# Inverting the chunk triangles of a gated DeltaNet in 32x32 tiles of TensorE

## The chip, the cores and the metric

One core of a Trainium2 chip. The metric is the device time of one execution in microseconds (us). Matmuls are float32 throughout. In the traces a float32 matmul leaves two pairs of records, a weight load (PEld) and a pass (PE) each; a transpose leaves one pair.

## The reference

One transformer layer for 2048 tokens of width 1024: modulation from a condition vector, one combined projection, a mix of latent attention (8 heads) and gated DeltaNet (4 heads of 128), an output projection, and a mixture of experts. The change is in the DeltaNet part, which solves a triangular system for each chunk of tokens and each head:

```python
lower = jnp.where(strict, jnp.einsum('bhncd,bhnsd->bhncs', k_beta, k) * decay, 0.0)
system = lower + jnp.eye(C, dtype=lower.dtype)
rhs = jnp.concatenate([v_beta, k_beta * jnp.exp(g)[..., None]], axis=-1)
sol = lax.linalg.triangular_solve(system, rhs, left_side=True, lower=True)
...
o_c = jnp.einsum('bhcd,bhde->bhce', q_c, state) + jnp.einsum('bhcs,bhse->bhce', a_c, v_new)
state = state * jnp.exp(gl_c)[..., None, None] + jnp.einsum('bhcd,bhce->bhde', kd_c, v_new)
```

The reference has chunks of 64 tokens. The kernel works on 16 chunks of 128 tokens, which gives the same outputs, so it inverts a unit triangular 128x128 matrix for each of 16 chunks and 4 heads.

## The kernel before

The kernel runs as stages one after another: `modulation`, `projection`, `mix`, `output`, `routing`, `experts`, `finish`. Only `mix` is touched. It does the attention and the DeltaNet together.

`mix_order` writes out one order of work. DeltaNet steps of chunk n (named K, KA, U0, W0, Y, WU, ...) stand in a list, each with a cost; attention atoms (S scores, X exponential, T transposes of the probabilities, V values, O output transposes) have costs of their own, 495.9 units in all. After each DeltaNet step so many atoms follow as its cost times a share pays for; the share is the sum of the atoms' costs over the sum of the steps' costs (380 units before). Every engine walks through this same order and does its part of each step. Within an engine the order is strict; between engines there are semaphores.

The steps of the inversion, for chunk n and all four heads at once (tiles of 128 partitions x 4 heads x 128):

- K: TensorE multiplies keys and queries (L1194), VectorE makes `lt` ("A_transposed", L1055), and GpSimd multiplies `lt` by the mask of each of seven levels into `xt` ("X_transposed", L905), 3 levels at K and the others after Y steps.
- U0: VectorE sets `U = I - X0` (L1068). W0: TensorE transposes U in 4 transposes (L1216), ScalarE copies it to `W` (L961).
- Levels 1 to 6, each in two steps. Y: 4 matmuls `X^T W` (L1226), ScalarE copies the result to `Y_all` (L965). WU: 4 matmuls for the update of W (L1235, levels 1 to 5 only) and 4 for that of U (L1238); VectorE subtracts both from `W` (L1089) and `U` (L1091).
- TR uses U: `vn = U^T R` (L1244), and the recurrence goes on with DS (L1250) and AV (L1255).

Other lines that the prediction names: M, one step a chunk, has four matmuls in column tiles of 32 (L1261); V has its two heads in column tiles of 64 (L1288); S is L1273, T is L1278. `at_bank` gives each step one or two of five PSUM banks.

Of the kernel before, what the change touches and what calls it, by code (L numbers as in the profile page):

```python
# [22 lines left out]
P = 128  # L23
F32, I32 = mybir.dt.float32, mybir.dt.int32
ALU = mybir.AluOpType
# [589 lines left out]
def mix_order():  # L615

    pairs = [(i, hp, b) for i in range(NT) for hp in range(AH // 2) for b in range(i // 4 + 1)]
    atoms = []
    for j, (i, hp, b) in enumerate(pairs):
        n = min(4, i + 1 - 4 * b)  # L620
        ahead = min(4, pairs[j + 1][0] + 1 - 4 * pairs[j + 1][2]) if j + 1 < len(pairs) else 0
        for e in range(2):
            atoms.append((0.11 * n, [("T", j, e)]))
            if ahead:
                atoms.append((0.22 * ahead, [("S", j + 1, e), ("X", j + 1, e)]))
        o = j - pairs.index((i, 0, 0))
        if i and o < AH // 2:
            atoms.append((0.11 * ((i - 1) // 4 + 1), [("O", i - 1, o)]))
        atoms.append((0.22 * n, [("V", j, 0)]))
        if i and o == AH // 2 - 1:  # L630
            atoms.append((0.0, [("A", i - 1, 0)]))
        if (hp, b) == (AH // 2 - 1, i // 4):
            atoms.append((0.0, [("B", i, 0)]))
    for o in range(AH // 2):
        atoms.append((0.44, [("O", NT - 1, o)]))
    atoms.append((0.0, [("A", NT - 1, 0)]))
    steps = []
    for c in range(-2, NT):
# [4 lines left out]
        steps += [(0.0, ("U0", n)), (0.7, ("W0", n)), (1.2, ("Y", n, 1))] * prep  # L643
# [3 lines left out]
        steps += [(1.35, ("WU", n, 2)), (1.2, ("Y", n, 3))] * prep  # L647
        steps += [(0.0, ("UTA", d))] * (d < NT)
        steps += [(1.35, ("WU", n, 3))] * prep
# [5 lines left out]
        steps += [(1.35, ("WU", n, 5))] * prep  # L655
        steps += [(0.0, ("O2", c))] * rec
        steps += [(1.2, ("Y", n, 6)), (0.5, ("WU", n, 6))] * prep
# [17 lines left out]
def mix(nc, m, a_log, dt_bias, w_mod, b_mod):  # L675

    LV = 7
    NLV = LV - 1
# [9 lines left out]
    with nc.cleanup_on_exit(), ExitStack() as ctx:  # L688
# [8 lines left out]
        masks = sb("level_masks", [P, LV, P])  # L697
# [4 lines left out]
        xt = sb("X_transposed", [P, 3, GH, P])  # L702
        U = [sb(f"U{i}", [P, GH, P]) for i in range(2)]
        at = [sb(f"qk_transposed{i}", [P, GH, P]) for i in range(2)]
        W, Y = sb("W_all", [P, GH, P]), sb("Y_all", [P, GH, P])
# [33 lines left out]
        xw_ready, y_copied, w_ready, u_ready, w_updated, u_updated = (sem(n) for n in (  # L739
            "xw_ready", "y_copied", "w_ready", "u_ready", "w_updated", "u_updated"))  # L740
# [12 lines left out]
        uses = {"G": 1, "K": 2, "VT": 1, "KD": 1, "KS": 2, "W0": 1, "Y": 1, "WU": 2, "TR": 1, "DS": 1, "AV": 1, "M": 1, "PRE": 2, "T": 1, "O": 1}  # L753
# [3 lines left out]
        for step in order:  # L757
            kind, n = step[0], step[1]
            if kind not in uses:
                continue  # L760
            lv = step[2] if len(step) > 2 else 0
            count = 1 if kind == "WU" and lv == NLV else uses[kind]
            held = sorted(range(NBANK), key=until.__getitem__)[:count]
            at_bank[step] = held
            bank_free[step] = [released[b] for b in held if released[b]]
            read = {"G": [(dm_ready, n + 1)], "K": [(at_ready, n + 1)] * 2, "VT": [(v_copied, n + 1)], "KD": [(kd_ready, n + 1)],
                    "KS": [(r_ready, n + 1), (qs_ready, n + 1)], "W0": [(w0_copied, n + 1)], "Y": [(y_copied, NLV * n + lv)],
                    "WU": [(u_updated, NLV * n + lv), (w_updated, (NLV - 1) * n + lv)], "TR": [(vn_ready, n + 1)],
                    "DS": [(state_ready, n + 1)], "AV": [(o_ready, n + 1)], "M": [(mod_added, n + 1)],
                    "PRE": [(pre, 14)] * 2,  # L770
                    "T": [(t_copied[lv % 2], n + 1)], "O": [(part_ready, n * (AH // 2) + lv + 1)]}[kind]
# [96 lines left out]
        def _(pool):  # L868
# [9 lines left out]
            for lv in range(LV):  # L878
# [16 lines left out]

            def level(n, lv):

                t = LV * n + lv
                if lv == 0:
                    wait(lt_ready, n + 1)  # L900
                if lv >= 3:
                    wait(u0_ready, n + 1) if lv == 3 else wait(xw_ready, NLV * n + lv - 3)
                else:
                    wait(xw_ready, NLV * (n - 1) + lv + 4)
                pool.tensor_tensor(xt[:, t % 3], lt[:], masks[:, lv].unsqueeze(1).to_broadcast([P, GH, P]), ALU.mult).then_inc(xt_ready, 1)  # L905

            for step in order:
# [26 lines left out]
        def _(act):  # L934
            wait = waiter(act)
            act.preload_act_table_set("natural_log_exp_and_others")
            for step in order:
# [20 lines left out]
                elif kind == "W0":  # L958
                    wait(w0_ready, n + 1)
                    wait(u_updated, NLV * n)  # L960
                    act.copy(W[:], bank[at_bank[step][0]][:]).then_inc(w0_copied, 1)  # L961
# [46 lines left out]
        def _(dve):  # L1008
# [3 lines left out]
            for step in order:  # L1012
# [36 lines left out]
                elif kind == "K":  # L1049
                    wait(kk_ready, n + 1)  # L1050
                    wait(em_ready, n + 1)
                    wait(xt_ready, n * LV)
# [4 lines left out]
                    last.then_inc(lt_ready, 1)  # L1057
                elif kind == "KA":
# [6 lines left out]
                elif kind == "U0":  # L1065
                    wait(xt_ready, n * LV + 1)
                    wait(tr_ready, n - 1)
                    dve.tensor_tensor(U[n % 2][:], m.ident[:].unsqueeze(1).to_broadcast([P, GH, P]), xt[:, (LV * n) % 3], ALU.subtract  # L1068
# [106 lines left out]
        def _(pe):  # L1175
            wait = waiter(pe)
            for step in order:
# [35 lines left out]
                elif kind == "W0":  # L1213
                    wait(u0_ready, n + 1)
                    for h in range(GH):
                        last = pe.transpose(bank[b0][:, h], U[n % 2][:, h], m.ident[:])  # L1216
                    last.then_inc(w0_ready, 1)
                elif kind == "Y":
                    lv = step[2]
                    wait(xt_ready, n * LV + 1 + lv)  # L1220
                    if lv == 1:
                        wait(w0_copied, n + 1)
                    else:
                        wait(w_updated, (NLV - 1) * n + lv - 1)
                    for h in range(GH):
                        last = pe.matmul(bank[b0][:, h], xt[:, (LV * n + lv) % 3, h], W[:, h], start=True, stop=True)  # L1226
                    last.then_inc(xw_ready, 1)
                elif kind == "WU":
                    lv = step[2]
                    wait(y_copied, NLV * n + lv)  # L1230
                    if lv > 1:
                        wait(u_updated, NLV * n + lv - 1)
                    if lv < NLV:
                        for h in range(GH):
                            last = pe.matmul(bank[b1][:, h], U[n % 2][:, h], Y[:, h], start=True, stop=True)  # L1235
                        last.then_inc(w_ready, 1)
                    for h in range(GH):
                        last = pe.matmul(bank[b0][:, h], Y[:, h], U[n % 2][:, h], start=True, stop=True)  # L1238
                    last.then_inc(u_ready, 1)
                elif kind == "TR":  # L1240
                    wait(r_ready, n + 1)
                    wait(u_updated, NLV * (n + 1))
# [829 lines left out]
```

## Time and profile before

| | |
|---|---|
| median of 3 runs | 2852.04 us (2846.66 to 2852.78) |
| the profiled execution | 2850.87 us, its span 2849.1 us |
| TensorE busy | 2533.8 us, 89% of the span |
| VectorE, ScalarE, GpSimd busy | 41%, 30%, 19% |
| granted TensorE clock, mean | 0.957 of 2.4 GHz |

The span is the time from the first to the last instruction of the profiled execution. The stage `mix` runs from about 800 to 1825 us of it. Busy time of TensorE is from the start of a pass to its modelled end, and passes overlap, so the price of an instruction is read from the distance between starts.

### The profile page before, as it was taken

How to read it: one execution, taken by the hardware profiler on the slowest of the kernel's cores; microseconds unless marked ns; L12 is line 12 of the kernel's file. 1: busy time of each engine (PE TensorE's matmuls, PEld its weight loads, DVE VectorE, ACT ScalarE, POOL GpSimd, SP SyncE). 2: the span in 40 equal slices, each digit the busy share in tenths (PEclk: the TensorE clock that was granted, in tenths of full speed). 3: DMA queues.
4: the chain of work that ended last, by engine and by line, in shares of the span. 5: the costliest groups of instructions: out<-in, count | busy, mean ns of one | idle time of the engine just before them, and what ended most of it. 6: DMA issues, size and time to landing. Idle time of an engine off the chain costs nothing. (4 is left out here: it accounts for less than half of the span.)

```text
span 2849.1 us, 37400 instructions
## 1 busy us (share of the span) xinstructions
PE 2533.8 (89%) x12276; PEld 1561.0 (55%) x12277; DVE 1167.4 (41%) x2349; ACT 855.6 (30%) x2023; POOL 539.1 (19%) x755
## 2 busy tenths in 40 slices
PE   7699999999959999999999999479993899999980
PEld 7354444444447777777777777345552444444440
DVE  0234334333336666666666656412225222222215
ACT  0225334252344444444444444221110011111102
POOL 0110000000022212221222221013331122222222
PEclk9999999999979999999999999789996899999995
DMA  7212112121163123111112111373330478999878
GB/s 261 75 52 69 54 56 76 35 70 39 50 189 94 60 67 105 62 51 47 51 40 71 62 35 35 135 273 119 118 118 22 128 211 266 286 314 309 233 196 361
DMA packets 194351, 348.60 MB, mean 122 GB/s; under 512 B 20368, under 2 KB 128912, under 8 KB 192032
## 3 DMA queue, kind: packets, MB, share of 16 engines
q1 hardware_dynamic: 180256, 296.39, 30.9%
q0 software_dynamic: 13952, 50.36, 7.3%
q8 instruction: 83, 1.36, 0.2%
q14 instruction: 60, 0.49, 0.1%
HBM read 246.56 MB, written 100.16 MB: 122 GB/s over the span
## 5 line engine op out<-in xcount | busy, mean ns | idle before, releaser
L604 PE MATMUL pV<-h_transposed,w_in_sb 128*128 128x512 f32 x768 | 337.6, 592 | 1.6 <-ACT h_transposed L399 1.6
L1900 PE MATMUL hidden_ps<-w,h_rowsT 128*128 x752 | 331.6, 594 | 0.0
L984 ACT ACTIVATE probs<-scores,neg_max 128x512 f32<-128x512 f32 (+3 forms) x320 | 199.5, 624 | 381.8 <-DVE neg_max L1130 258.9
L1273 PE MATMUL scores<-keys,queries 96*128 96x512 f32 (+3 forms) x640 | 289.2, 534 | 13.3 <-DMA values<-v_d 13.3
L1900 PEld LDWEIGHTS hidden_ps<-w,h_rowsT 128*128 128x128 f32 x752 | 143.3, 191 | 180.3 <-issue 180.2
L604 PEld LDWEIGHTS pV<-h_transposed,w_in_sb 128*128 128x128 f32 x768 | 144.6, 190 | 174.8 <-issue 169.8
L1490 PE MATMUL out_ps<-w_out_sb,yT 128*128 128x512 f32 x512 | 225.7, 599 | 2.2 <-DVE yT L1463 2.2
L905 POOL TENSOR_TENSOR X_transposed<-A_transposed,level_masks 128x512 f32<-128x512 f32 x112 | 141.1, 1272 | 409.0 <-DVE A_transposed L1055 196.1
L1278 PE MATMUL bank<-ident,probs 128*128 128x128 f32 x1088 | 178.9, 280 | 3.6 <-ACT probs L984 2.7
L1130 DVE TENSOR_REDUCE neg_max<-scores 128x1 f32<-128x512 f32 x192 | 132.4, 690 | 105.0 <-PE scores L1273 104.0
L1910 PE MATMUL expert_ps<-w_sb,hiddenT 128*128 x368 | 169.8, 604 | 0.0
L1278 PEld LDWEIGHTS bank<-ident,probs 128*128 128x128 f32 x1088 | 127.2, 141 | 74.4 <-issue 69.4
L1288 PE MATMUL outT_ps<-probs_T,values 128*64 128x128 f32 x2176 | 155.5, 281 | 11.7 <-issue 5.9
L1490 PEld LDWEIGHTS out_ps<-w_out_sb,yT 128*128 128x128 f32 x512 | 96.8, 192 | 118.8 <-issue 116.0
L1830 ACT ACTIVATE silu_gate<-hidden_ps 128x256 f32<-128x256 f32 x47 | 18.1, 385 | 454.4 <-PE hidden_ps L1900 454.4
L1288 PEld LDWEIGHTS outT_ps<-probs_T,values 128*64 128x64 f32 x2176 | 116.9, 137 | 68.5 <-issue 55.8
L1859 DVE TENSOR_TENSOR hidden<-silu_gate,hidden_ps 128x256 f32<-128x256 f32 x47 | 19.8, 422 | 276.3 <-ACT silu_gate L1830 276.3
L522 DVE TENSOR_SCALAR conv_acc<-conv_in,conv_taps 128x512 f32<-128x512 f32 x48 | 23.7, 494 | 243.4 <-ACT conv_in L441 243.4
L1868 DVE SCALAR_TENSOR_TENSOR expert_y<-expert_ps,slot_gate,mod_rows 128x512 f32<-128x512 f32 x92 | 64.8, 747 | 133.2 <-PE expert_ps L1910 133.2
L1273 PEld LDWEIGHTS scores<-keys,queries 96*128 96x128 f32 x640 | 99.8, 194 | 26.5 <-issue 25.0
L560 PE MATMUL pG<-w_in_sb,h_transposed 128*128 128x512 f32 x256 | 112.5, 592 | 0.0
L1226 PE MATMUL bank<-W_all,X_transposed 128*128 128x128 f32 x768 | 104.4, 279 | 7.2 <-ACT W_all L961 4.8
(334 smaller groups left out, 3905.9 us busy)
## 6 DMA issues: line engine op xcount, KB each, us to landing
w<-in_w_dram SPq DMA_DIRECT2D x64, 1024.0 KB, 10.8
w_sb<-in_w_dram SPq DMA_DIRECT2D x32, 1024.0 KB, 14.1
w_mod_rows<-in_w_mod_dram SPq DMA_DIRECT2D x16, 1024.0 KB, 4.8
kqv<-qkv_d SPq DMA_DIRECT2D x16, 768.0 KB, 4.7
y_d<-diag_mask SPq DMA_DIRECT2D x17, 512.0 KB, 6.0
mod_w<-in_w_mod_dram SPq DMA_DIRECT2D x2, 4096.0 KB, 21.7
x_in<-in_x_dram SPq DMA_DIRECT2D x16, 512.0 KB, 3.6
qkv_d<-l_out SPq DMA_DIRECT2D x32, 256.0 KB, 2.3
```

Of the source, the lines that this page charges most:

```text
L560: last = pe.matmul(pG[:], hT[:, n // ST % 2, k, n % ST * P:(n % ST + 1) * P], win[:, k, GATE0:], start=(k == 0), stop=(k == ND - 1))
L604: last = pe.matmul(pV[n % 2][:], win[:, k, QKV0 + c * P:QKV0 + (c + 1) * P], hT[:, s % 2, k, :], start=(k == 0), stop=(k == ND - 1))
L905: pool.tensor_tensor(xt[:, t % 3], lt[:], masks[:, lv].unsqueeze(1).to_broadcast([P, GH, P]), ALU.mult).then_inc(xt_ready, 1)
L984: act.activation(prob[:, e, 0:w].rearrange("p t k -> p (t k)"), pS[e][:, 0:w * P], ACT.Exp, scale=-1.0, bias=nmin[:, i % 2, h, b:b + 1], a ...
L1130: dve.tensor_reduce(nmin[:, i % 2, h, b:b + 1], pS[e][:, 0:w], AX.X, ALU.min).then_inc(min_ready, 1)
L1226: last = pe.matmul(bank[b0][:, h], xt[:, (LV * n + lv) % 3, h], W[:, h], start=True, stop=True)
L1273: pe.matmul(pS[e][:, 0:w * P], qT[:, i % 2, h], kT[:, 4 * b:4 * b + w, h, :], start=True, stop=True).then_inc(s_ready, 1)
L1278: last = pe.transpose(bank[b0][:, t], prob[:, e, t], m.ident[:])
L1288: last = pe.matmul(pO[64 * e:64 * e + 64, n % 4], v[:, 4 * b + t, h * DV:(h + 1) * DV], probT[:, n % 2, e, t], start=(t == 0), stop=(t == ...
L1490: last = pe.matmul(pX[:, half], yT[par][:, k], wo[:, k, half * 512:(half + 1) * 512], start=(k == 0), stop=(k == ND - 1))
L1900: last = pe.matmul(pH[par][:], xT[par][:, k], m.w13[:, ds(slot, 1), k].rearrange("p s n -> p (s n)"), start=(k == 0), stop=(k == ND - 1))
L1910: last = pe.matmul(pY[:, half], hT[par][:, k], m.w2b[:, ds(slot, 1), k, half * 512:(half + 1) * 512].rearrange("p s n -> p (s n)"), start= ...
```

## The change

The inversion of the 128x128 triangle is cut by block size. Levels 0 to 4 stay inside diagonal blocks of 32, so they now work on a compact form: for each head the four diagonal 32x32 blocks stand under each other in 128 partitions x 32 columns. VectorE copies these blocks out of `lt` into `ltb` (four copies), GpSimd makes all five masked levels in two instructions, and TensorE multiplies each block in its own 32x32 tile of the array (rows q and columns q for block q). W and U stand side by side in one tile `WU`, so one subtraction updates both. W0 is a matmul by a compact identity in place of a transpose.

Level 5 joins pairs of blocks of 32 to blocks of 64, level 6 the two of 64 to 128, each on its off-diagonal block alone. A new ScalarE step D copies the finished blocks into the wide `U` and into `Wh`; level 5's result is written by three ScalarE instructions, level 6's by one of VectorE. `U` and `Wh` are zeroed once at the start. The costs of the Y and WU steps in `mix_order` are lowered, so that all steps sum to 307.2 units.

```diff
-        steps += [(1.35, ("WU", n, 1)), (1.2, ("Y", n, 2))] * prep
+        steps += [(0.9, ("WU", n, 1)), (0.8, ("Y", n, 2))] * prep
...
-        steps += [(1.2, ("Y", n, 4))] * prep
+        steps += [(0.8, ("Y", n, 4)), (0.9, ("WU", n, 4)), (0.0, ("D", n))] * prep
         steps += [(0.85, ("G", d))] * (d < NT)
-        steps += [(1.35, ("WU", n, 4)), (1.2, ("Y", n, 5))] * prep
+        steps += [(0.8, ("Y", n, 5))] * prep
...
-    LV = 7
-    NLV = LV - 1
+    NLV = 6
+    LVB, BL = 5, 32
+    quarter = [slice(BL * j, BL * (j + 1)) for j in range(P // BL)]
...  GpSimd
                 elif kind == "K":
-                    for lv in range(3):
-                        level(n, lv)
-                elif kind == "Y" and step[2] + 2 < LV:
-                    level(n, step[2] + 2)
+                    wait(ltb_ready, n + 1)
...
+                    pool.tensor_tensor(xt[:, 0], ltb[:], mask_b[:, 0].unsqueeze(1).to_broadcast([P, GH, BL]), ALU.mult).then_inc(xt_ready, 1)
+                    pool.tensor_tensor(xt[:, 1:], ltb[:].unsqueeze(1).to_broadcast([P, LVB - 1, GH, BL]),
+                                       mask_b[:, 1:].unsqueeze(2).to_broadcast([P, LVB - 1, GH, BL]), ALU.mult).then_inc(xt_ready, 1)
...  ScalarE
-                    act.copy(Y[:], bank[at_bank[step][0]][:]).then_inc(y_copied, 1)
+                    bk = bank[at_bank[step][0]]
+                    if step[2] < LVB:
+                        act.copy(Yb[:], bk[:, :, 0:BL]).then_inc(y_copied, 1)
+                    elif step[2] == LVB:
+                        act.copy(Yb[quarter[1]], bk[quarter[1], :, 0:BL])
+                        act.copy(Yb[quarter[3]], bk[quarter[3], :, 0:BL]).then_inc(y_copied, 1)
+                    else:
+                        act.copy(Yh[64:], bk[64:, :, 0:64]).then_inc(y_copied, 1)
+                elif kind == "D":
...
+                    for q in quarter[0:2]:
+                        act.copy(Wh[q, :, q], WU[q, :, 0])
+                    for q in quarter[2:4]:
+                        last = act.copy(U[n % 2][q, :, q], WU[q, :, 1])
+                    last.then_inc(diag_ready, 1)
+                    for q in quarter[0:2]:
+                        last = act.copy(U[n % 2][q, :, q], WU[q, :, 1])
+                    last.then_inc(diag_ready, 1)
+                elif kind == "WU" and step[2] == LVB:
...
+                    act.activation(Wh[quarter[1], :, quarter[0]], bk[quarter[1], :, 0:BL], ACT.Copy, scale=-1.0)
+                    act.activation(U[n % 2][quarter[2], :, quarter[3]], bk[quarter[2], :, 0:BL], ACT.Copy, scale=-1.0)
+                    act.activation(U[n % 2][quarter[0], :, quarter[1]], bk[quarter[0], :, 0:BL], ACT.Copy, scale=-1.0).then_inc(quarter_done, 1)
...  VectorE
+                    wait(lt_ready, n + 1)
+                    for q in quarter:
+                        last = dve.tensor_copy(ltb[q], lt[q, :, q])
+                    last.then_inc(ltb_ready, 1)
...
-                elif kind == "WU":
-                    lv = step[2]
-                    if lv < NLV:
-                        wait(w_ready, (NLV - 1) * n + lv)
-                        dve.tensor_tensor(W[:], W[:], bank[at_bank[step][1]][:], ALU.subtract).then_inc(w_updated, 1)
-                    wait(u_ready, NLV * n + lv)
-                    dve.tensor_tensor(U[n % 2][:], U[n % 2][:], bank[at_bank[step][0]][:], ALU.subtract).then_inc(u_updated, 1)
+                elif kind == "WU" and step[2] < LVB:
+                    wait(u_ready, NLV * n + step[2])
+                    dve.tensor_tensor(WU[:], WU[:], bank[at_bank[step][0]][:, :, 0:2 * BL].rearrange("p h (two c) -> p h two c", two=2),
+                                      ALU.subtract).then_inc(u_updated, 1)
+                elif kind == "WU" and step[2] == NLV:
+                    wait(u_ready, NLV * (n + 1))
+                    dve.tensor_scalar(U[n % 2][0:64, :, 64:], bank[at_bank[step][0]][0:64, :, 0:64], -1.0, None, ALU.mult
+                                      ).then_inc(half_done, 1)
...  TensorE, Y and WU
                     for h in range(GH):
-                        last = pe.matmul(bank[b0][:, h], xt[:, (LV * n + lv) % 3, h], W[:, h], start=True, stop=True)
+                        if lv < LVB:
+                            for q in quarter:
+                                last = pe.matmul(bank[b0][q, h, 0:BL], xt[q, lv, h], WU[q, h, 0], start=True, stop=True)
+                        elif lv == LVB:
+                            for first, second in (quarter[0:2], quarter[2:4]):
+                                last = pe.matmul(bank[b0][second, h, 0:BL], lt[first, h, second], WU[first, h, 0], start=True, stop=True)
+                        else:
+                            last = pe.matmul(bank[b0][64:, h, 0:64], lt[0:64, h, 64:], Wh[:, h], start=True, stop=True)
...
-                    if lv < NLV:
-                        for h in range(GH):
-                            last = pe.matmul(bank[b1][:, h], U[n % 2][:, h], Y[:, h], start=True, stop=True)
-                        last.then_inc(w_ready, 1)
                     for h in range(GH):
-                        last = pe.matmul(bank[b0][:, h], Y[:, h], U[n % 2][:, h], start=True, stop=True)
+                        if lv < LVB:
+                            for q in quarter:
+                                pe.matmul(bank[b0][q, h, 0:BL], WU[q, h, 1], Yb[q, h], start=True, stop=True)
+                            for q in quarter:
+                                last = pe.matmul(bank[b0][q, h, BL:2 * BL], Yb[q, h], WU[q, h, 1], start=True, stop=True)
+                        elif lv == LVB:
+                            pe.matmul(bank[b0][quarter[1], h, 0:BL], WU[quarter[1], h, 1], Yb[quarter[1], h], start=True, stop=True)
+                            for first, second in (quarter[0:2], quarter[2:4]):
+                                last = pe.matmul(bank[b0][first, h, 0:BL], Yb[second, h], WU[second, h, 1], start=True, stop=True)
+                        else:
+                            last = pe.matmul(bank[b0][0:64, h, 0:64], Yh[64:, h], U[n % 2][64:, h, 64:], start=True, stop=True)
```

## Rows read from the trace of the kernel before

**Rows 1.** The page: busy time, then TensorE and its granted clock in 40 slices.

```profile
PE 2533.8 (89%) x12276; PEld 1561.0 (55%) x12277; DVE 1167.4 (41%) x2349; ACT 855.6 (30%) x2023; POOL 539.1 (19%) x755
...
PE   7699999999959999999999999479993899999980
...
PEclk9999999999979999999999999789996899999995
```

**Rows 2.** Windows: busy us of each engine, granted clock, DMA share; `mix` and its end.

```profile
core 0: us, PE busy (x) PEld busy (x) DVE busy (x) ACT busy (x) POOL busy (x), PEclk, DMA share, GB/s
860.00:1820.00 960.00, 918.59 (x7151) 705.28 (x7151) 614.50 (x1328) 438.80 (x1182) 202.74 (x195) 1.00 0.19 60
1820.00:1880.00 60.00, 14.98 (x34) 7.41 (x35) 5.57 (x9) 10.45 (x12) 0.81 (x2) 0.58 0.80 282
```

**Rows 3.** Waits inside `mix`, longest in total first: us, times, longest.

```profile
PE bank L1216 <- DVE U L1068: 13.2, 11, 1.6
...
PE bank L1226 <- ACT W_all L961: 4.8, 7, 1.3
```

**Rows 4.** Timeline of TensorE: start us, length, line, passes (x).

```profile
1401.30 1.05 PE L1250 MATMUL bank<-v_new,k_to_end 128*128 128x128 f32 x8
1402.28 1.09 PE L1288 MATMUL outT_ps<-probs_T,values 128*64 128x128 f32 x16
1403.31 0.66 PE L1278 MATMUL bank<-ident,probs 128*128 128x128 f32 x4
1403.80 1.06 PE L1235 MATMUL bank<-Y_all,U 128*128 128x128 f32 x8
1404.69 1.06 PE L1238 MATMUL bank<-U,Y_all 128*128 128x128 f32 x8
1405.59 1.02 PE L1273 MATMUL scores<-keys,queries 96*128 96x512 f32 x2
1406.45 0.60 PE L1278 MATMUL bank<-ident,probs 128*128 128x128 f32 x4
```

**Rows 5.** Timeline of TensorE around a step M (L1261).

```profile
1058.92 0.66 PE L1278 MATMUL bank<-ident,probs 128*128 128x128 f32 x4
1059.51 1.07 PE L1261 MATMUL bank<-w_mod_rows,c_padded 128*32 128x512 f32 x8
1060.50 1.13 PE L1273 MATMUL scores<-keys,queries 96*128 96x512 f32 x2
1061.46 0.60 PE L1278 MATMUL bank<-ident,probs 128*128 128x128 f32 x4
1061.90 1.06 PE L1235 MATMUL bank<-Y_all,U 128*128 128x128 f32 x8
```

**Rows 6.** Timelines of that M over its first 0.01, 0.03 and 0.5 us.

```profile
1059.51 0.62 PE L1261 MATMUL bank<-w_mod_rows,c_padded 128*32 128x512 f32 x1
...
1059.51 0.64 PE L1261 MATMUL bank<-w_mod_rows,c_padded 128*32 128x512 f32 x4
...
1059.51 0.16 PEld L1261 LDWEIGHTS bank<-w_mod_rows,c_padded 128*32 128x32 f32 x8 [0.17 <-issue]
```

**Rows 7.** Timelines of weight loads after a wait: the first, then the first two.

```profile
1116.27 0.13 PEld L1288 LDWEIGHTS outT_ps<-probs_T,values 128*64 128x64 f32 x1 [0.99 <-issue]
...
1116.27 0.17 PEld L1288 LDWEIGHTS outT_ps<-probs_T,values 128*64 128x64 f32 x2 [0.99 <-issue]
```

**Rows 8.** Groups of VectorE in `mix`, by form: busy us, mean ns, idle before.

```profile
L1091 DVE TENSOR_TENSOR U<-U,bank 128x512 f32<-128x512 f32 x96 | 65.9, 686 | 23.2 <-PE bank L1238 22.9
L1089 DVE TENSOR_TENSOR W_all<-W_all,bank 128x512 f32<-128x512 f32 x80 | 54.9, 686 | 36.8 <-PE bank L1235 36.0
L1062 DVE TENSOR_TENSOR qk_transposed<-bank,decay 128x256 f32<-128x256 f32 x32 | 11.9, 413 | 0.0
L1068 DVE TENSOR_TENSOR U<-ident,X_transposed 128x512 f32<-128x512 f32 x16 | 10.9, 683 | 0.1
L1135 DVE COPY probs_T<-bank 128x128 f32<-128x128 f32 x16 | 4.5, 284 | 0.7 <-PE bank L1278 0.6
```

**Rows 9.** Groups of ScalarE in `mix`, by form.

```profile
L965 ACT COPY Y_all<-bank 128x512 f32<-128x512 f32 x96 | 55.7, 580 | 13.1 <-PE bank L1226 12.8
L996 ACT COPY out_T<-outT_ps 128x128 f32<-128x128 f32 x160 | 42.1, 263 | 47.3 <-PE outT_ps L1288 47.0
L970 ACT ACTIVATE v_new<-bank,beta 128x128 f32<-128x128 f32 x64 | 18.2, 370 | 1.6 <-PE bank L1244 1.6
L961 ACT COPY W_all<-bank 128x512 f32<-128x512 f32 x16 | 9.7, 603 | 8.4 <-PE bank L1216 8.4
```

**Rows 10.** The group of GpSimd in `mix` that the change touches.

```profile
L905 POOL TENSOR_TENSOR X_transposed<-A_transposed,level_masks 128x512 f32<-128x512 f32 x112 | 141.1, 1272 | 409.0 <-DVE A_transposed L1055 196.1 <-PE bank L1226 113.8 <-DVE U L1068 99.0
```

More of the change, by code:

```diff
@@ L696, in mix @@
         eg, neg_eg, etot, ekd = (sb(n, [P, NT * GH]) for n in ("exp_g", "neg_exp_g", "exp_total", "exp_to_end"))
-        masks = sb("level_masks", [P, LV, P])
+        masks, mask_b, ident_b = sb("level_masks", [P, LVB, P]), sb("block_masks", [P, LVB, BL]), sb("block_ident", [P, BL])
         kq = [sb(f"kqv{i}", [P, NC, P]) for i in range(2)]
@@ L701, in mix @@
         lt = sb("A_transposed", [P, GH, P])
-        xt = sb("X_transposed", [P, 3, GH, P])
+        ltb, xt = sb("A_blocks", [P, GH, BL]), sb("X_transposed", [P, LVB, GH, BL])
         U = [sb(f"U{i}", [P, GH, P]) for i in range(2)]
         at = [sb(f"qk_transposed{i}", [P, GH, P]) for i in range(2)]
-        W, Y = sb("W_all", [P, GH, P]), sb("Y_all", [P, GH, P])
+        WU, Yb = sb("W_U_blocks", [P, GH, 2, BL]), sb("Y_blocks", [P, GH, BL])
+        Wh, Yh = sb("W_half", [P // 2, GH, P // 2]), sb("Y_half", [P, GH, P // 2])
         R, kd, o, vn = (sb(n, [P, GH, P]) for n in ("v_then_residual", "k_to_end", "q_state_then_out", "v_new"))
@@ L738, in mix @@
             "av_ready", "ds_ready", "state_ready", "o_ready", "osq_ready", "oss_ready", "o_pow", "yg_ready", "yg_stored"))
-        xw_ready, y_copied, w_ready, u_ready, w_updated, u_updated = (sem(n) for n in (
-            "xw_ready", "y_copied", "w_ready", "u_ready", "w_updated", "u_updated"))
+        xw_ready, y_copied, u_ready, u_updated = (sem(n) for n in ("xw_ready", "y_copied", "u_ready", "u_updated"))
+        ltb_ready, diag_ready, quarter_done, half_done, mask_b_made, zero_made = (sem(n) for n in (
+            "ltb_ready", "diag_ready", "quarter_done", "half_done", "mask_b_made", "zero_made"))
         modw_loaded, mod_ready, mod_added, bias_loaded, mod_stored, bias_zero, zeros_stored = (sem(n) for n in (
@@ L761, in mix @@
             lv = step[2] if len(step) > 2 else 0
-            count = 1 if kind == "WU" and lv == NLV else uses[kind]
-            held = sorted(range(NBANK), key=until.__getitem__)[:count]
+            held = sorted(range(NBANK), key=until.__getitem__)[:uses[kind]]
             at_bank[step] = held
@@ L877, in _ @@
             n_mask = 0
-            for lv in range(LV):
+            for z in (U[0], U[1], Wh):
+                pool.memset(z[:], 0.0).then_inc(zero_made, 1)
+            for lv in range(LVB):
                 b = 1 << lv
@@ L894, in _ @@
             pool.wait_ge(mask_step, n_mask)
[L896 to L905, printed above, removed]
+            pool.wait_ge(zero_made, 3)
             for step in order:
@@ L959, in _ @@
                     wait(w0_ready, n + 1)
-                    wait(u_updated, NLV * n)
-                    act.copy(W[:], bank[at_bank[step][0]][:]).then_inc(w0_copied, 1)
+                    act.copy(WU[:, :, 0], bank[at_bank[step][0]][:, :, 0:BL]).then_inc(w0_copied, 1)
                 elif kind == "Y":
@@ L964, in _ @@
                     wait(u_ready, NLV * n + step[2] - 1)
-                    act.copy(Y[:], bank[at_bank[step][0]][:]).then_inc(y_copied, 1)
+                    bk = bank[at_bank[step][0]]
[7 more added lines that the diff above has]
+                elif kind == "D":
+                    wait(u_updated, (LVB - 1) * (n + 1))
+                    wait(xw_ready, NLV * n)
+                    wait(tr_ready, n - 1)
+                    act.wait_ge(zero_made, 3)
+                    for q in quarter[0:2]:
[7 more added lines that the diff above has]
+                elif kind == "WU" and step[2] == LVB:
+                    wait(u_ready, NLV * n + LVB)
+                    wait(xw_ready, NLV * n)
+                    wait(tr_ready, n - 1)
+                    bk = bank[at_bank[step][0]]
+                    act.activation(Wh[quarter[1], :, quarter[0]], bk[quarter[1], :, 0:BL], ACT.Copy, scale=-1.0)
+                    act.activation(U[n % 2][quarter[2], :, quarter[3]], bk[quarter[2], :, 0:BL], ACT.Copy, scale=-1.0)
+                    act.activation(U[n % 2][quarter[0], :, quarter[1]], bk[quarter[0], :, 0:BL], ACT.Copy, scale=-1.0).then_inc(quarter_done, 1)
                 elif kind == "TR":
@@ L1051, in _ @@
                     wait(em_ready, n + 1)
-                    wait(xt_ready, n * LV)
+                    wait(xt_ready, 2 * n)
+                    wait(xw_ready, n * NLV)
+                    if n == 0:
+                        dve.wait_ge(mask_step, 3 * LVB)
+                        dve.tensor_reduce(mask_b[:], masks[:].rearrange("p l (q c) -> p l c q", c=BL), AX.X, ALU.add).then_inc(mask_b_made, 1)
+                        dve.tensor_reduce(ident_b[:], m.ident[:].rearrange("p (q c) -> p c q", c=BL), AX.X, ALU.add).then_inc(mask_b_made, 1)
                     both = [bank[b] for b in at_bank[step]]
@@ L1065, in _ @@
                 elif kind == "U0":
-                    wait(xt_ready, n * LV + 1)
-                    wait(tr_ready, n - 1)
-                    dve.tensor_tensor(U[n % 2][:], m.ident[:].unsqueeze(1).to_broadcast([P, GH, P]), xt[:, (LV * n) % 3], ALU.subtract
+                    wait(xt_ready, 2 * n + 1)
+                    wait(mask_b_made, 2)
+                    wait(u_ready, NLV * (n - 1) + LVB)
+                    wait(diag_ready, 2 * n)
+                    dve.tensor_tensor(WU[:, :, 1], ident_b[:].unsqueeze(1).to_broadcast([P, GH, BL]), xt[:, 0], ALU.subtract
                                       ).then_inc(u0_ready, 1)
@@ L1215, in _ @@
                     for h in range(GH):
-                        last = pe.transpose(bank[b0][:, h], U[n % 2][:, h], m.ident[:])
+                        for q in quarter:
+                            last = pe.matmul(bank[b0][q, h, 0:BL], WU[q, h, 1], ident_b[q], start=True, stop=True)
                     last.then_inc(w0_ready, 1)
@@ L1241, in _ @@
                     wait(r_ready, n + 1)
-                    wait(u_updated, NLV * (n + 1))
+                    wait(half_done, n + 1)
+                    wait(diag_ready, 2 * n + 2)
                     for h in range(GH):
```

27 lines of the change are left out of this document (16 added, 11 removed).

## The prediction

> **What bounds the kernel now.** I read the page first [rows 1]: TensorE is at 90% or more in nearly every slice, VectorE at 41% of the span, ScalarE at 30%. The change touches only the stage `mix`, so I asked for windows there [rows 2]. From 860 to 1820 us TensorE is busy 918.6 of 960 us at the full clock (2.4 GHz level), VectorE 614.5 (64%), ScalarE 438.8 (46%). Then the list of waits [rows 3]: TensorE waits for the inversion's own chain in few places, 13.2 us in total for U before W0 and 4.8 for W before Y. So the attention atoms between the steps hide the latency of that chain, and `mix` takes what TensorE's queue of instructions takes. Whatever shortens that queue shortens the stage, until the waits show. The window behind the stage waits for transfers that start when `mix` ends, so it moves along with it.
>
> **What the inversion costs TensorE now.** I take prices from distances between starts. L1235 starts at 1403.80 and L1238 at 1404.69: 8 passes (4 matmuls) of 128 columns take 0.89 us, 0.111 a pass [rows 4]. Transposes have one pass each: L1278 at 1406.45 would be followed after 4 x 0.11 = 0.44, as 1061.46 to 1061.90 shows [rows 5]. A chunk has W0 (0.44), six Y (0.89 each) and eleven groups in WU (5 x 2 + 1, 0.89 each): 0.44 + 17 x 0.89 = 15.57 us. With 16 chunks that is 249 us of the stage.
>
> **What it costs after.** Matmuls per chunk: W0 16, Y of levels 1 to 4 64, WU of levels 1 to 4 128, Y5 8, WU5 12: 228 in 32x32 tiles. Y6 and WU6: 8 in 64x64 tiles. No row shows a 32x32 tile, so the price p of one of the 228 has to be bounded.
>
> - A pass of 512 columns takes 0.43 us (L1273, 0.86 for two [rows 4]), one of 128 takes 0.111; so 32 columns take about 0.027, and a matmul, with two passes, 0.054 in its own tile.
> - M has four column tiles of 32, and they run side by side: its 8 passes of 512 columns take 0.99 us, where one tile alone would take 0.86 and four after another 3.4 [rows 5]. Its first four passes start within 0.02 us, and all eight loads lie within 0.16, of which 0.11 is the length of one [rows 6]: about 0.007 a pass when the queue is full. If the four diagonal tiles run side by side too, four matmuls take 0.054, and p is 0.0135. This is the lower bound.
> - After a wait, with the queue empty, the second weight load of V starts 0.04 us behind the first (0.17 less 0.13) [rows 7]. If every matmul has to be brought up at this pace, p is 0.04. WU now brings 32 matmuls at a time, so part of each group will go at such a pace. This is the upper bound as long as tiles overlap.
>
> I take p = 0.022: near the middle, toward the full queue, since the steps on either side (0.86 to 1.1 us for 2 to 16 passes) give the queue time to fill. 228 x 0.022 = 5.0 us. Y6 and WU6: 8 matmuls x 2 passes x 64 columns (0.053) = 0.86 us.
>
> **Changing the tile.** M and V show that entering another tile shape costs time. The 4 transposes ahead of M take 0.59 in place of 0.44, of which 0.05 is owed to the V before them; M itself takes 0.99 in place of 0.86; and the scores behind it 0.96 in place of 0.86 [rows 5]. V's entry lengthens L1250 from 0.89 to 0.98, V takes 1.03 for 8 pairs of passes (0.87), and the transposes behind it 0.49 [rows 4]. That is some 0.3 us for one visit to another shape and back, 0.34 at most and, where the neighbour is a V that has to change anyway, about half. There are 13 visits a chunk (W0, six Y, six WU); the lowered costs still owe at least 0.8 x 495.9/307.2 = 1.29 units of atoms after each, more than any single atom, so each stands alone. I take 13 x 0.25 = 3.25 us, bounds 0.19 and 0.34.
>
> **Waits.** The cover in units of atoms after a Y falls from 1.2 x 1.30 = 1.57 to 1.29, after a WU from 1.76 to 1.45. The work that it hides shrinks too: ScalarE's copy goes from 0.58 us (512 elements) to 0.26 (128) [rows 9], VectorE's from 2 x 0.69 to one of 256 elements, 0.41 [rows 8]. So the slack stays about the same in levels 1 to 4. It is thinner in two places. D puts six copies of 0.26, 1.6 us in a row, on ScalarE, and queued behind them are exponentials and the copies of T, for which TensorE's T and V wait. WU5 is followed by three ScalarE writes of 0.26 to 0.37 with about 1.5 us of cover ahead of Y6. I put 0.5 us a chunk, bounds 0 and 1.
>
> **The other engines.** VectorE loses L1091, L1089 and L1068, 131.7 us, and gains 64 updates of 0.41, 16 of 64x256 at about the same, 16 of 0.28 for U0, and 64 block copies of 0.28: about 56 us [rows 8]. ScalarE loses 65 us and gains 16 x (one copy for W0, four for Y, two for Y5, six in D, three in WU5 at 0.26 to 0.37, one of 256 elements), about 76 us [rows 9]. GpSimd loses 141 us [rows 10] and gains under 30. In the stage after, VectorE would be busy about 540 of 865 us and ScalarE 450: neither becomes the bound, so none of this enters the sum. The chain ahead of W0 gets the block copies (1.1 us) but loses most of a 1.27 us mask product and 0.4 of U0; at nothing, with its cover of atoms from K to W0. If that cover were gone it would cost up to 1.1 us a chunk. The start of the stage has three memsets more, six mask instructions fewer and two reductions: within 1 us of nothing.
>
> **The sum.** After: 5.0 + 0.86 + 3.25 + 0.5 = 9.6 us a chunk, against 15.57: 5.95 saved, x 16 = 95 us. The profiled execution took 2850.87 us (1.8 more than its span, 1.2 less than the median), so about 2756 us. With all low bounds (3.08 + 0.86 + 2.47 = 6.4) it is 147 us less, 2704; with all high ones (9.1 + 0.86 + 4.4 + 1.0 = 15.4) 3 us less, 2848.
>
> **Against the trace: two rules.** V has a sustained pace of 1.03 us for 8 matmuls, and M starts passes 0.007 us apart, with column tiles that share one bank [rows 4, 6]. The Trainium skill says in TensorEngine Tiling (Array Packing), under Gotcha 1: PSUM Pressure, that different row tiles cannot access the same PSUM bank at once; the four diagonal tiles here differ in rows and all write one bank. No row shows this case, since M and V tile columns only; by that rule the four would go one after another. The skill's TensorE: Matmul & The Clock Gate, under Back-to-back issue gap, names about 62 ns for each MATMUL where its instructions are decoded in software; by it the 228 matmuls would take 14.1 us, the sum would be 18.7 and the time about 2901. The pace in rows 6 and 7 is below that figure, so this trace speaks against it.
>
> **The rivals.**
>
> - Tiles of different rows don't overlap (or a group can't be fed). Then p is 0.054: 12.3 + 0.86 + 3.25 + 0.5 = 16.9 us, 1.35 more than before, +22 us: 2872. It decides from p = (15.57 - 4.61)/228 = 0.048 on. For it: no row shows row tiles. Against: column tiles overlap fully [rows 6]. 15 in 100.
> - The queue gets shorter but the waits take it back: D and the three writes hold up ScalarE, and TensorE, in order, stands before T, V or Y6. At half the saving it is 2803 us; the case covers 2795 to 2850. For it: ScalarE's work grows while the stage shrinks. Against: idle time of TensorE is 4% now, and ScalarE was under half busy [rows 2]. 20 in 100.
> - The granted clock falls to its 1.2 GHz level in parts of `mix`, as it does in the window behind it, where TensorE is busy 15 of 60 us (mean 0.58). If a tenth of TensorE's 865 us ran so, +87 us, about 2843. Against: now the stage holds the full level, and atoms stand between all the small groups [rows 2]. 3 in 100.
> - More than forecast (the lower bounds hold): 2700 to 2715. 6 in 100.
>
> **Chances.** The forecast, 2715 to 2795, has 56 in 100. A range from 2710 to 2840 leaves out the slow rival, most of the clock's case and the edge of the last one, under 20 in 100. A measurement of this kernel can tell about 0.2% (6 us) from no change. Faster by more than that: the forecast, the better case and most of the second rival, 0.79. Within it: 0.05. Slower: 0.16.
>
> **What would show it.** The L-groups of Y and WU should start their next neighbour 0.5 to 0.7 us later (Y) and 0.8 to 1.1 (WU, levels 1 to 4). Passes of one head in the four tiles should start within 0.03 us. TensorE's idle time in `mix` should stay under 60 us and the stage should end near 1720 to 1740. If passes of 32 columns start 0.027 or more apart, the slow rival is right; if TensorE waits for `U`, `W_half` or probs_T for over 3 us a chunk, the second is.

## The result and the profile after

The changed kernel takes 2765.3 us (median of 4, 2759.42 to 2768.62) against 2850.62: ratio 0.9697, 95% interval 0.9684 to 0.971, 85 us less. The forecast was 2756 with a range of 2710 to 2840. All times of experiments below are medians, and their ratios are to the kernel before, run beside them. One execution of experiment 5 (3345.92 us) and one of run 10 (5463.15 us) were slow and are left out of the ratios; the medians given include them and would be 2765.69 and 2731.73 us without.

The page after (busy time, the slices of TensorE and its clock, the instruction queue of the DMA), and the window that answers to [rows 2]:

```profile
PE 2422.3 (88%) x17588; PEld 1407.8 (51%) x17589; DVE 1087.8 (39%) x2319; ACT 867.1 (31%) x2183; POOL 425.2 (15%) x672
...
PE   7699999999968899999999999299982999999980
...
PEclk9999999999977999999999999699995999999995
...
q8 instruction: 124, 2.03, 0.3%
```

```profile
core 0: us, PE busy (x) PEld busy (x) DVE busy (x) ACT busy (x) POOL busy (x), PEclk, DMA share, GB/s
860.00:1724.00 864.00, 807.55 (x12218) 555.70 (x12218) 531.25 (x1292) 453.14 (x1347) 96.38 (x120) 0.99 0.22 67
```

TensorE's last instruction of `mix` ends near 1725 us where it ended near 1816, 91 us earlier. TensorE's busy time fell by 111.5 us over the whole span, its idle time inside the window grew from 41 (960 less 918.6, of which some 3 lie behind the stage) to 56 us. VectorE and ScalarE did about what the prediction counted (531 and 453 us).

The timeline of TensorE after, with a WU of level 1 to 4 and a Y; it answers to [rows 4]:

```profile
1301.43 0.60 PE L1330 MATMUL bank<-ident,probs 128*128 128x128 f32 x4
1301.97 0.26 PE L1281 MATMUL bank<-Y_blocks,W_U_blocks 32*32 32x32 f32 x8
1302.05 0.24 PE L1283 MATMUL bank<-W_U_blocks,Y_blocks 32*32 32x32 f32 x8
1302.12 0.24 PE L1281 MATMUL bank<-Y_blocks,W_U_blocks 32*32 32x32 f32 x8
...
1302.48 0.24 PE L1283 MATMUL bank<-W_U_blocks,Y_blocks 32*32 32x32 f32 x6
1302.65 1.13 PE L1325 MATMUL scores<-keys,queries 96*128 96x512 f32 x2
1303.61 0.49 PE L1347 MATMUL bank<-ident,out_T 128*128 128x128 f32 x3
1304.04 0.45 PE L1268 MATMUL bank<-W_U_blocks,X_transposed 32*32 32x32 f32 x32
1304.42 1.09 PE L1340 MATMUL outT_ps<-probs_T,values 128*64 128x128 f32 x16
```

The 64 passes of the WU take 0.68 us from start to next start (1301.97 to 1302.65), where two groups took 1.79; the 32 of the Y take 0.38 in place of 0.89. Eight passes start in 0.07 us, which one tile alone would need 0.22 for (8 x 0.027), so the four diagonal tiles do run side by side. The price of the visit stands around them: the transposes before the WU take 0.54 in place of 0.44, and the scores behind it 0.96 in place of 0.86.

### The profile page after: what moved, and what is told of

Read it like the earlier page. It is cut to its first block and busy times, and to the rows that moved or that the text cites. A ratio compares the mean times of both kernels' runs of the same rounds, so it can differ in the third digit from the quotient of the medians.

```text
span 2757.7 us, 48101 instructions
## 1 busy us (share of the span) xinstructions
PE 2422.3 (88%) x17588; PEld 1407.8 (51%) x17589; DVE 1087.8 (39%) x2319; ACT 867.1 (31%) x2183; POOL 425.2 (15%) x672
## 5 line engine op out<-in xcount | busy, mean ns | idle before, releaser
L1325 PE MATMUL scores<-keys,queries 96*128 96x512 f32 (+3 forms) x640 | 303.5, 557 | 14.1 <-DMA values<-v_d 14.1
L525 DVE SCALAR_TENSOR_TENSOR conv_acc<-conv_in,conv_taps,conv_acc 128x512 f32<-128x512 f32 x144 | 108.5, 753 | 5.1
L1962 PEld LDWEIGHTS expert_ps<-w_sb,hiddenT 128*128 128x128 f32 x368 | 66.1, 189 | 69.2 <-issue 66.0
```

The lines of the kernel that those rows point to most:

```text
L525: dve.scalar_tensor_tensor(out=acc[:, b, :], in0=raw[:, b, j:j + SW], scalar=taps[:, c, j:j + 1], in1=acc[:, b, :], op0=ALU.mult, op1=ALU. ...
L1325: pe.matmul(pS[e][:, 0:w * P], qT[:, i % 2, h], kT[:, 4 * b:4 * b + w, h, :], start=True, stop=True).then_inc(s_ready, 1)
L1962: last = pe.matmul(pY[:, half], hT[par][:, k], m.w2b[:, ds(slot, 1), k, half * 512:(half + 1) * 512].rearrange("p s n -> p (s n)"), start= ...
```

## Experiments

**Theories.** The first (the prediction's): four tiles overlap, a small matmul is cheap (0.0135 to 0.04 us), and what keeps the gain from being larger is the 13 visits a chunk plus some waits. Rivals: the small matmuls are cheap for another reason, such as the pace of instructions; ScalarE's queue holds TensorE up; the order of work is what moves the time.

**1. The same tile again and again.** In W0, Y and WU of levels 1 to 4 the loops are swapped:

```diff
-                    for h in range(GH):
-                        for q in quarter:
+                    for q in quarter:
+                        for h in range(GH):
```

> The changed kernel with the loops over blocks and heads swapped in W0, Y and WU of levels 1 to 4, so that four (in WU eight) matmuls in a row go to the same 32x32 tile. If the price of a small matmul comes from the four tiles working side by side (0.38 us for the 32 passes of a Y, 0.68 us for the 64 of a WU in the changed kernel), a tile used again at once has to finish two passes of about 0.027 us first: 16 x 0.054 = 0.86 us for a Y, 1.7 for a WU, some 6 us more a chunk, about +95 us, so about 2860 us (ratio to before about 1.00). If instead the pace is that at which instructions come to TensorE, nothing changes: 2765 us.

Measured 2871.88 us, ratio 1.0093 (1.0067 to 1.012). Here is the same pair of steps in its timeline, the WU first (rows left out are its passes):

```profile
1303.43 0.24 PE L1284 MATMUL bank<-Y_blocks,W_U_blocks 32*32 32x32 f32 x2
1303.51 0.22 PE L1285 MATMUL bank<-W_U_blocks,Y_blocks 32*32 32x32 f32 x2
1303.58 0.22 PE L1284 MATMUL bank<-Y_blocks,W_U_blocks 32*32 32x32 f32 x2
...
1305.26 1.13 PE L1330 MATMUL scores<-keys,queries 96*128 96x512 f32 x2
1306.32 0.89 PE L1268 MATMUL bank<-W_U_blocks,X_transposed 32*32 32x32 f32 x32
1307.14 0.88 PE L1345 MATMUL outT_ps<-probs_T,values 128*64 128x128 f32 x12
```

The WU takes 1.83 us and the Y 0.82: 0.057 and 0.051 a matmul, the forecast's 0.054 for a tile by itself. The same matmuls in another order cost 107 us and turn the gain into a loss of 0.9%. This is the state that the prediction's slow rival described: overlap of the tiles is what the change lives on.

**2. All small matmuls of W0, Y and WU (levels 1 to 4) twice.** Each `for q in quarter` becomes `for q in quarter + quarter`.

> The changed kernel with each 32x32 matmul of W0, Y and WU of levels 1 to 4 issued twice (208 more a chunk, no more changes of tile shape, the results the same). It measures the price p of one more small matmul by itself. If p is about 0.016 as the starts in the changed kernel suggest, +53 us: about 2818 us. If it is the 0.022 of the prediction, +73 us: 2838. If the clusters were cheap only because the queue had been filled ahead, and a longer one falls to the pace of an empty queue, 0.04: +130 us.

Measured 2900.5 us, ratio 1.0168 (1.0153 to 1.0183): +135 us, 0.041 for each of 3328 extra matmuls. The passes themselves came as fast as before (0.017 a matmul, 57 us), but its timeline has pauses in the middle of clusters, for which the trace names no releaser:

```profile
1083.33 0.26 PE L1283 MATMUL bank<-W_U_blocks,Y_blocks 32*32 32x32 f32 x9
1085.95 0.25 PE L1283 MATMUL bank<-W_U_blocks,Y_blocks 32*32 32x32 f32 x5 [2.36 <-issue]
```

There are 54 pauses of over 0.08 us inside clusters of small tiles, 58.5 us in all; the changed kernel has 5, 7 us in all. The clock takes a part too: this execution's stage (it took 2912 us, 12 above the median) spends 92 us at the 1.2 GHz level from 860 us on, the changed kernel's 20, which is at most 36 us of work lost. Its page counts the instruction transfers:

```profile
q8 instruction: 176, 2.88, 0.4%
```

83 packets of 16 KB before, 124 after the change, 176 here.

**3. Only W0 and Y twice.**

> As the run that doubled all small matmuls, but only W0 and Y of levels 1 to 4 are doubled: 80 more matmuls a chunk, 1280 in all, so that no cluster is longer than the 64 passes of a WU. The run that doubled all paid 0.041 us for each extra matmul, and its trace had 54 pauses of about 1 us inside clusters. If the pauses come from clusters long enough to use up instructions faster than they are brought to TensorE, short doubles cost only the 0.017 us of their passes: +21 us, 2787. If 0.041 is the price of any further small matmul, +52 us: 2817.

Measured 2796.91 us, ratio 0.9819 (0.9804 to 0.9834): +31.6 us, 0.025 each. Its doubled Y takes 0.68 us for 64 passes, so 16 more matmuls take 0.30: 0.0188 each, 24 us of the 31.6. It has 10 pauses, 13 us. So the passes of one more matmul cost 0.017 to 0.019, and the rest grows faster than their number, with the pauses. Experiment 1 has the changed kernel's instructions at a third of the pace, and one pause of 0.26 us.

The traces' records of DMA packets tie the pauses to the instruction queue. All 54 of experiment 2 end 1.20 to 1.72 us after the end of one of its 16 KB packets (median 1.41), the 5 of the changed kernel 1.30 to 1.51, nine of the 10 here 1.09 to 1.57 and the tenth 2.32, while the packets come 6.9 us apart (154 between 812 and 1880 us in experiment 2). Their number follows TensorE's records: 52 more packets for 13312 more passes and weight loads, 256 for each packet. So in these pauses TensorE stands for instructions that have not arrived. Why the packets come too late was not tested: no run changed the supply alone.

**4. Extra visits.** In TR, DS and AV, ahead of each of the four matmuls:

```diff
                     for h in range(GH):
+                        pe.matmul(bank[b0][0:BL, h, 0:BL], ident_b[0:BL], ident_b[0:BL], start=True, stop=True)
                         last = pe.matmul(bank[b0][:, h], kd[:, h], vn[:, h], start=True, stop=True)
```

> The changed kernel with one matmul of a constant 32x32 block ahead of each of the four matmuls in TR, DS and AV: 12 more visits to the small tile shape a chunk, 192 in all, at almost no work of their own (0.054 us each). The constant's result is overwritten. If a visit costs 0.3 us, as the prediction reads from M and V, +10 +58 = about +65 us: 2830 us. If it costs 0.2, +45 us: 2810. If changing the shape costs nothing and the missing gain is all in waits, +10 us or less: 2775.

Measured 2828.17 us, ratio 0.9922 (0.9908 to 0.9937): +63 us for 192 visits, 0.33 each; less the two passes (0.054), a visit costs 0.27.

**5. D on GpSimd.** The six copies and their waits move from ScalarE's queue to GpSimd's, with waits for GpSimd's own earlier instructions.

> The changed kernel with the six block copies of step D on GpSimd in place of ScalarE. If the waits behind D on ScalarE's queue are part of what the change loses (TensorE waits for probs and probs_T behind it), this gives 5 to 15 us: 2750 to 2760. If ScalarE is not in the way, the time stays at 2765 within 4 us, or gets worse if GpSimd's copies come too late for level 6 or hold up its own part of G.

Measured 2765.9 us, ratio 0.9697 (0.9684 to 0.971): no change. ScalarE's load at D is not what TensorE waits for.

**6. Levels 5 and 6 alone**, on the kernel before; levels 1 to 4 stay full width:

```diff
                     for h in range(GH):
-                        last = pe.matmul(bank[b0][:, h], xt[:, (LV * n + lv) % 3, h], W[:, h], start=True, stop=True)
+                        if lv < 5:
+                            last = pe.matmul(bank[b0][:, h], xt[:, (5 * n + lv) % 3, h], W[:, h], start=True, stop=True)
+                        elif lv == 5:
+                            for first, second in (quarter[0:2], quarter[2:4]):
+                                last = pe.matmul(bank[b0][second, h, 0:32], lt[first, h, second], W[first, h, first], start=True, stop=True)
+                        else:
+                            last = pe.matmul(bank[b0][64:, h, 0:64], lt[0:64, h, 64:], W[0:64, h, 0:64], start=True, stop=True)
...
```

> The kernel before with one part of the change alone: levels 5 and 6 on their off-diagonal blocks (8 and 12 matmuls in 32x32 tiles, 4 and 4 in 64x64 tiles), levels 1 to 4 full width as before, the order of work unchanged. From the slots of TensorE in the two traces: levels 5 and 6 take 4.45 us a chunk before and 1.94 after, and four visits to small tiles lengthen their neighbours by about 0.75, so 1.76 us a chunk, -28 us: 2823 us. If the visits ate up the gain of so few matmuls it would be 2850; if the two levels carried most of the change's gain, 2790.

Measured 2814.57 us, ratio 0.988 (0.9865 to 0.9895): -35 us, 7 more than expected. Four visits and 28 small matmuls a chunk bring two fifths of the gain; nine visits and 208 matmuls bring the rest.

**7. The costs of before in the order of work.**

> The changed kernel with the costs of the Y and WU steps in the order of work as they were before (380 units in all). If the waits that are left come from the thinner cover behind Y and WU steps (1.29 and 1.45 units in place of 1.57 and 1.76), this gives back some 5 to 10 us: 2757. If the longer stretches without a step elsewhere (K, KS, TR, DS, AV get less cover) cost as much, the time stays at 2765 or rises by 5 to 10.

Measured 2754.04 us, ratio 0.967 (0.9657 to 0.9684), 8 to 11 us less than the changed kernel; the intervals meet at 0.9684. What differs is the granted clock, here in two windows of the changed kernel and the same two of this one:

```profile
860.00:920.00 60.00, 50.07 (x666) 35.73 (x667) 31.76 (x97) 29.07 (x87) 6.70 (x10) 0.91 0.35 99
1220.00:1280.00 60.00, 57.91 (x821) 39.98 (x820) 34.46 (x80) 29.59 (x88) 6.42 (x8) 0.94 0.19 59
```

```profile
860.00:920.00 60.00, 50.88 (x785) 35.93 (x785) 33.23 (x103) 30.77 (x94) 6.69 (x10) 1.00 0.38 112
1220.00:1280.00 60.00, 57.14 (x827) 39.25 (x826) 36.35 (x87) 30.38 (x89) 7.19 (x10) 1.00 0.23 70
```

TensorE's idle time up to the end of the stage is 54.6 us here (858 - 803.4), 56.4 in the changed kernel, so it is not the waits: the gain has the size that was expected, but not its reason. A mean of 0.91 over 60 us is 11 us at the 1.2 GHz level, 0.94 another 7. The effect is small and not settled: run 11 finds nothing of it.

**8. Y next to V.** Ahead of each Y, atoms are drawn forward until a V is next; the Y comes right before it.

> The changed kernel with another order: each Y is put directly ahead of a V where one is near, so that 147 sides of the 208 small clusters touch a V (whose column tiles need a change of shape anyway) in place of 71, and some WU follow right behind that V. By the price of a visit 76 sides save about 0.1 us each, -8 us: 2757. If ScalarE's copy of Y comes too late behind the short V, TensorE waits and it is the same or slower, 2765 to 2785.

Measured 2791.57 us, ratio 0.9796 (0.9782 to 0.9809): 26 us slower. Its waits name the reason, times in us, how often, and the longest:

```profile
PE bank L1292 <- ACT Y_blocks L974: 17.4, 22, 1.9
...
PE bank L1300 <- ACT Y_half L979: 10.1, 11, 1.6
```

These two were 3.8 and 3.4 us in the changed kernel. A V of 1.03 us does not cover ScalarE's copy. Half a visit saved at each of 76 sides would have been worth 10 us (76 x 0.135), and these two waits took 20; all of TensorE's idle time in the stage grew from 56 to 90 us (897 less 806.7).

**9 to 11. Fewer visits and fewer matmuls.** VectorE can transpose each 32x32 block of a tile. Run 9 makes W0 so, and needs neither TensorE nor ScalarE for it; run 10 makes W anew from U at each of the levels 1 to 4 too. Both have the costs of experiment 7, run 11 those of the changed kernel:

```diff
+                    wait(u0_ready, n + 1)
+                    dve.transpose(WU[:, :, 0], WU[:, :, 1]).then_inc(w0_copied, 1)
...
-                            for q in quarter:
-                                pe.matmul(bank[b0][q, h, 0:BL], WU[q, h, 1], Yb[q, h], start=True, stop=True)
...
+                    dve.tensor_tensor(WU[:, :, 1], WU[:, :, 1], bank[at_bank[step][0]][:, :, 0:BL], ALU.subtract).then_inc(u_step, 1)
+                    wait(u_step, (LVB - 1) * n + step[2])
+                    dve.transpose(WU[:, :, 0], WU[:, :, 1]).then_inc(u_updated, 1)
```

> The changed kernel with the costs of before in the order of work (2754 us by itself) and without the visit W0: W0 is the transpose of U0 in each 32x32 block, which VectorE can do alone, right behind U0, in one instruction on 128 elements a partition. It takes away 16 of 208 visits, each a slot of 0.38 us and about 0.2 on the neighbours, and one ScalarE copy of 0.26 us, 0.6 us a chunk: -9 us, and TensorE's waits for U0 ahead of W0 (9 us in the trace) in part: 2740 us. If TensorE only waits elsewhere for the same chain, 2750.

Run 9 measured 2746.04 us, ratio 0.9631 (0.9618 to 0.9643), 8 us under experiment 7.

> As the run before it, and W is made from U by the same VectorE transpose at each of the levels 1 to 4 too, so that a WU has 16 matmuls and not 32 (64 fewer matmuls a chunk, 1024 in all) and VectorE has two instructions of 128 elements for one of 256. The number of visits stays. At 0.017 us a matmul -17 us against that run: about 2723 us. If the gain of fewer small matmuls is eaten by the longer chain on VectorE (U, its own wait, the transpose), 2740 or more.

Run 10 measured 2731.84 us, ratio 0.9573 (0.9561 to 0.9586), 14 us less again: 1024 matmuls at 0.014 us.

> As the run before it, with the lower costs of the changed kernel in the order of work in place of those of before. If the higher costs help by the cover behind each small cluster, as the run with the old costs suggests (11 us), this is some 10 us slower than the run before it, about 2733 us. With W made on VectorE a WU is half as long; if the costs should follow TensorE's time, the lower ones are right now, and it is equal or faster.

Run 11 measured 2729.59 us, ratio 0.9569 (0.9557 to 0.9582), no different from run 10. It is the fastest version found, 36 us under the changed kernel, from which it differs in the transposes alone.

## Why the prediction was right

The direction, the mechanism and the size held: 85 us against 95. By its steps:

- **TensorE sets the time of `mix`.** Right. TensorE stays at 93% of its window, and experiments 1 to 4, which only slow TensorE's queue or add to it, all show up in the time.
- **p = 0.022 us for a small matmul.** A little high. A Y of 16 matmuls takes 0.38 us and one of 32 takes 0.68, so p is 0.019; the doubled WU, where it has no pause, gives 0.017. At 0.018 the 208 of levels 0 to 4 take 3.7 us a chunk. The 20 of level 5, which the prediction priced the same, rotate over two and three tiles only: their two slots take 0.37 and 0.38 us, as long as the 16 of a Y. So all 228 take at most 4.5 us in place of 5.0, 8 us in all. The lower bound of 0.0135 was not reached, since passes follow at 0.0083 to 0.0088 us and not at 0.007. The upper one (0.04, from an empty queue) did not show even behind a wait: six WU that start after waits of over 0.2 us take 0.67 us, no longer than the others. The mean price of 0.041 in experiment 2 has another cause, the pauses and the clock.
- **Y6 and WU6 at 0.86.** Too low: each takes 0.605 us up to the next start, 1.21 together. Part of that is the price of the visit, which the prediction counts in the next term.
- **13 visits at 0.25.** Right: 0.27 by experiment 4, 3.5 us a chunk in place of 3.25. They cost nearly as much as all the small matmuls together. The prediction's 1.29 units of atoms after every visit do not hold for W0 (cost 0.7) and WU6 (0.5), which are owed 1.13 and 0.81; all the same, no two of the 208 clusters stand side by side in the trace. The Trainium skill, TensorEngine Tiling (Array Packing), section Key Properties, says that a change of the tiling mode drains TensorE; this case agrees, with those 0.27 us for in and out.
- **Waits at 0.5 us a chunk.** Too low; this term used up what the others gave. From 860 us to the end of the stage, at 1815 and 1724 us, TensorE's busy time fell by 109.5 us (917.1 to 807.6), 6.8 a chunk, where the forecast without its waits has 6.5 (15.57 less 9.11). Its idle time grew from 37.9 us (955 less 917.1) to 56.4 (864 less 807.6), 1.2 a chunk. The pauses inside clusters are 6 us of that. D and its six copies, named as the thin place, were not it (experiment 5). The line that grew most is V's wait, before and after, for which the view names no releaser:

```profile
PE outT_ps L1288 <- issue: 5.9, 10, 1.1
```

```profile
PE outT_ps L1340 <- issue: 14.5, 18, 1.6
```

The longest-held V shows what it stands for, after:

```profile
1500.49 0.91 DVE L1089 COPY A_blocks<-A_transposed 32x128 f32<-32x128 f32 x4
1501.43 0.69 DVE L1171 COPY probs_T<-bank 128x512 f32<-128x512 f32 x1
...
1502.22 0.62 PE L1340 MATMUL outT_ps<-probs_T,values 128*64 128x128 f32 x7 [1.64 <-issue]
```

All 18 of these waits end 0.1 us after VectorE's copy of the probabilities (L1171), and so do the 10 before (L1135). At four of the 18, 5 us together, the new block copies (L1089) stand in VectorE's queue within 2 us ahead of it. The prediction left VectorE out of the sum because it is not the bound (61% busy in the stage after); its order of work holds TensorE up all the same. What the block copies cost was not tested by a run.

- **The clock at no cost.** Not quite: from 860 us on, the changed kernel's stage spends 20 us at the lower level, the kernel before 7. That is at most 7 us of work lost.
- **The rivals.** Tiles one after another: refuted by the trace after and given its price by experiment 1 (2872 us, as worked out). That it fits to the microsecond is luck: the sum has nothing for the clock, and that run's stage spends 52 us at the lower level, the kernel before 7. The rule in Gotcha 1: PSUM Pressure of the Trainium skill's TensorEngine Tiling (Array Packing), that row tiles cannot use one PSUM bank at once, does not bind tiles that differ in rows and columns: four of them write one bank with starts 0.007 us apart. The 62 ns a MATMUL of the Trainium skill's TensorE: Matmul & The Clock Gate, Back-to-back issue gap, stated there for decoding in software, do not show here either: 32 matmuls took 0.68 us. Waits that take the gain back: in part, as above; experiment 8 shows how fast they do so once the cover shrinks.
- **Its signs.** The stage ended at 1725 us, idle time stayed under 60, and four tiles started within 0.03 us, as named. The neighbours of Y and WU start sooner than named, after 0.38 and 0.68 us in place of 0.5 to 0.7 and 0.8 to 1.1: of the visit's price some 0.2 us falls on the steps on either side, and the signs counted it in the slot.

## What to carry to other kernels

Small tiles pay when successive matmuls go to different tiles: the same 208 matmuls a chunk are a 3% gain in one loop order and a 1% loss in the other. Count a fixed price for each visit to another tile shape (0.27 us here) and set it against what the cluster saves; then look for clusters that need not exist, as a transpose of 32x32 blocks on an engine with room did here for 36 us. Long clusters of tiny matmuls can outrun their instructions: doubling their number cost more than twice their passes (0.041 us a matmul), while halving it in the WU gave back the passes alone (0.014). And count the queue of an engine that is far from full, where the busy one waits for its next copy.

## What the runs showed of the hardware

- Pauses of 0.2 to 4.6 us inside clusters without any wait, 5 in the changed kernel and 54 with twice the small matmuls, while the instruction queue of the DMA went from 124 to 176 packets of 16 KB. All 59 end 1.2 to 1.7 us after the end of such a packet.
- Passes of 32 columns in four diagonal tiles start 0.007 us apart, in rounds of about 0.03. With two tiles in the rotation the round is as long: the 8 matmuls of level 5's Y take 0.37 us, the 16 of another Y 0.38. On one tile two passes take 0.051 to 0.057 us.
- The granted clock fell to the 1.2 GHz level in short stretches of the stage, from 860 us on 7 us in the kernel before, 20 in the changed one, 7 in experiment 7 and 41 in experiment 8, 52 in experiment 1 and 92 in experiment 2. Runs 9 and 10 have 34 and 38 and are faster all the same. Two of the changed kernel's stretches, at 890 and 1241 us, began at waits of about 2 us. The timeline of TensorE at the second one:

```profile
1238.91 0.60 PE L1330 MATMUL bank<-ident,probs 128*128 128x128 f32 x4
1241.42 0.65 PE L1268 MATMUL bank<-W_U_blocks,X_transposed 32*32 32x32 f32 x32 [1.91 <-ACT W_U_blocks L957]
```

The Y behind the wait takes 0.58 us up to the next start (1242.00) in place of 0.38. So one wait costs more than its length. That it was the wait that brought the clock down was not tested.
